# Rotary embedding by VectorE's lane shuffle in place of a rotation matrix on TensorE, in two of three chained transformer blocks

## The reference

```python
def apply_axial_rope(t, cos, sin):            # block 1: queries and keys
    tr = t.reshape(B, L, H, 2, 2, ROPE_PAIRS)  # ROPE_PAIRS = 16
    t1, t2 = tr[..., 0, :], tr[..., 1, :]
    out = jnp.stack([t1 * cs - t2 * sn, t2 * cs + t1 * sn], axis=-2)

def _rope(x, pos):                             # block 2: queries, compressed, selected and window keys
    x1, x2 = xf[..., :half], xf[..., half:]    # half = 32 of 64 channels
    return jnp.concatenate([x1 * cos - x2 * sin, x2 * cos + x1 * sin], axis=-1)
```

## Time and profile before

| | |
|---|---|
| times of three runs | 2611.19, 2609.15, 2611.22 us (median 2611.19) |
| profiled execution's own time | 2606.98 us |
| its span in the profile | 2605.2 us |
| busy PE, DVE, ACT, POOL | 2383.5 (91%), 1247.3 (48%), 976.5 (37%), 281.6 us (11%) |
| moved by the DMA queues | 884.58 MB, mean 340 GB/s |

### The profile page before, as it was taken

How to read it: one execution, slowest core, us unless ns; L and a number is a source line. 1 busy time by engine, 2 the same in 40 slices (tenths; PEclk the granted TensorE clock), 3 DMA queues, 4 the chain that set the end, 5 groups by cost and what they waited for, 6 DMA issues and landing times.

```text
span 2605.2 us, 43248 instructions
## 1 busy us (share of the span) xinstructions
PE 2383.5 (91%) x16141; PEld 1553.9 (60%) x16142; DVE 1247.3 (48%) x3094; ACT 976.5 (37%) x2122; POOL 281.6 (11%) x270
## 2 busy tenths in 40 slices
PE   7999989999999999999999998988778877799998
PEld 5679965555555545555568798443222322288997
DVE  2554542222222222222225757776666666557775
ACT  3343332112212121122124545554444444455774
POOL 0000000000000000000000001444434444200000
PEclk9999999999999999999999999999999999999999
DMA  6676699999999998999966655999999999833453
GB/s 271 263 262 252 228 358 417 422 422 422 421 422 422 422 422 355 422 422 422 422 236 266 258 226 218 422 421 421 421 422 421 421 421 422 361 133 138 162 185 139
DMA packets 121701, 884.58 MB, mean 340 GB/s; under 512 B 13536, under 2 KB 13536, under 8 KB 14304
## 3 DMA queue, kind: packets, MB, share of 16 engines
q1 hardware_dynamic: 83520, 607.16, 58.1%
q0 software_dynamic: 38048, 275.60, 25.5%
HBM read 881.66 MB, written 1.05 MB: 339 GB/s over the span
## 4 chain that ended last, share of the span: by engine, by line
PE 65%; DMA 22%; ACT 5%; DVE 3%; issue 2%; SPq 2%; POOL 0%; ACTq 0%; DVEq 0%; POOLq 0%
PE psum L840 15%; PE psum L1148 14%; DMA work<-in_uv,work 12%; PE psum L1526 8%; PE psum L1180 6%; DMA work<-in_stream 5%; DMA weight_ring<-in_stream 5%; PE psum L1619 2%; PE psum L1094 2%; PE psum L1115 2%; PE psum L693 2%; PE psum L863 2%; PE psum L913 2%; SPq L1689 2%; PE psum L753 1%
## 5 line engine op out<-in xcount | busy, mean ns | idle before, releaser
L1526 PE MATMUL psum<-work 128*128 128x512 f32 x1024 | 499.1, 620 | 116.9 <-ACT work L3302 116.0
L1526 PEld LDWEIGHTS psum<-work 128*128 128x128 f32 x1024 | 180.1, 192 | 426.8 <-ACT work L3302 273.0
L2503 DVE CUSTOM_DVE_ANT_0 work<-work 128x1024 f32<-128x1024 f32 x256 | 313.5, 1225 | 213.2 <-DMA work<-in_uv,work 211.9
L2144 DVE TENSOR_TENSOR work<-psum,work 128x256 f32<-128x256 f32 x132 | 56.0, 424 | 695.6 <-PE psum L1126 695.6
L1148 PE MATMUL psum<-work 128*64 128x256 f32 x3168 | 367.2, 383 | 17.3 <-DMA work<-in_stream 13.0
L1774 DVE TENSOR_TENSOR ring_parts<-weight_ring,peer_parts 128x1024 fp32r<-128x1024 f32 x218 | 261.4, 1221 | 200.6 <-ACT peer_parts L2935 155.3
L2935 ACT ACTIVATE peer_parts<-weight_ring 128x1024 fp32r<-128x1024 f32 x218 | 224.2, 1052 | 259.4 <-DMA weight_ring<-in_stream 157.2
L3492 POOL DMA_INDIRECT work<-in_uv,work x256 | 275.9, 1078 | 379.3 <-PE psum L1526 324.2
L1148 PEld LDWEIGHTS psum<-work 128*64 128x64 f32 x3168 | 220.6, 137 | 154.5 <-issue 29.3
L1180 PE MATMUL psum<-weight_ring,work 128*64 128x512 f32 x1056 | 244.2, 599 | 28.6 <-ACT work L3111 25.2
L3093 ACT ACTIVATE work<-psum 128x256 f32<-128x256 f32 x132 | 50.7, 384 | 366.9 <-PE psum L1148 366.9
(11 more groups left out here) (376 smaller groups left out, 3249.8 us busy)
## 6 DMA issues: line engine op xcount, KB each, us to landing
weight_ring<-in_stream SPq DMA_DIRECT2D x322, 1024.0 KB, 7.5
work<-in_stream SPq DMA_DIRECT2D x192, 1024.0 KB, 22.8
chunkbuf<-in_stream SPq DMA_DIRECT2D x64, 1024.0 KB, 22.7
work<-in_uv,work POOLq DMA_INDIRECT x256, 22.7
work<-in_rows POOLq DMA_DIRECT2D x1, 1312.0 KB, 15.0
xT<-in_x POOLq DMA_DIRECT2D x1, 1024.0 KB, 12.0
work<-in_ctx POOLq DMA_DIRECT2D x1, 1024.0 KB, 9.9
work<-in_keys POOLq DMA_DIRECT2D x1, 1024.0 KB, 7.5
```

Of the source, the lines that this page charges most:

```text
L1526: mm = pe.matmul(psum[:, 2 * t + h, :], m["diag"][:, g % DIAGS, :], m["rows_of_uv"][row_place[g]][:, D + h * 512:D + (h + 1) * 512], start ...
L2144: ve.tensor_tensor(tb, psum[:, 6, 0:256].rearrange("p (q k) -> p q k", q=4), m["b_gu"][:, slice(b0, b0 + 4) if q is None else bass.ds(b0, ...
L2503: ve.tensor_tensor_reduce(row, row, m["h_nat"][:, t, :], 1.0, 0.0, ALU.mult, ALU.add, m["score"][:, g:g + 1]).then_inc(pick_s, 1)
```

## The change

`rotate` and its matrix go. DVE's `rope` starts from `raw` directly: a stream shuffle writes `raw` into `t2` with lanes 0 to 15 and 16 to 31 of every 32 lanes swapped; `t1 = raw*cos` follows; then, after waits for DVE's own results, `t2 = t2*sin` and the sum. The minus sign is in the sine table. Since the shuffle stays within 32 lanes, block 2's head channels are put into another order (`paired`) on the host, in the weights that make the queries and keys and in the tables that go with them, so that partners there are 16 lanes apart too. Nine PE products of 128x512 or 128x256 go, and nine banks fewer are opened (five in block 1, four in block 2). The tables are 128 columns shorter in both blocks.

```diff
-    1: [("cos", T), ("sin", T), ("rot", P), ("mask", 2 * P), ...
+    1: [("cos", T), ("sin", T), ("mask", 2 * P), ...
+SWAPPED = [(lane + 16) % 32 for lane in range(32)]
...
-            def rotate(tag, E, m, raw, n0, n):
-                pe.wait_ge(*at(f"raw:{tag}"))
-                ps = bank(f"rot:{tag}")
-                pe.matmul(ps[:, 0:n * T], m["r"]["rot"], raw[:, n0:n0 + n, :], start=True, stop=True) \
-                  .then_inc(*E.up(f"rot:{tag}"))
...
                 for i in range(4):
                     columns_of_parts(1, "q1", i, m["h_high"], h_low)
-                    if i == 0:
-                        rotate("k1", E, m, m["kraw"], 0, 2)
-                    else:
-                        rotate(f"q1:{i - 1}", E, m, m["qraw"], 2 * (i - 1), 2)
-                rotate("q1:3", E, m, m["qraw"], 6, 2)
...
-                rotate("k2a", E, m, m["kraw"], 0, 2)
-                rotate("k2b", E, m, m["kraw"], 2, 1)
                 of_h = m["h_high"], h_low
                 pe.wait_ge(*at("high:h2"))
                 columns_of_parts(2, "hq", 0, *of_h, late="h2_parts")
-                for i in range(2):
-                    rotate(f"q2:{i}", E, m, m["qraw"], 2 * i, 2)
...
             def rope(tag, V, m, raw, dst, n0, n, *names):
-                ve.wait_ge(*at(f"rot:{tag}"))
+                ve.wait_ge(*at(f"raw:{tag}"))
                 wait_own(V)
-                ps = bank_of(f"rot:{tag}")[:, 0:n * T].rearrange("p (j t) -> p j t", j=n)
...
-                tt(V, m["t1"][:, 0:n, :], raw[:, n0:n0 + n, :], cos, ALU.mult)
-                tt(V, m["t2"][:, 0:n, :], ps, sin, ALU.mult, f"free:rot:{tag}")
+                t1, t2 = m["t1"][:, 0:n, :], m["t2"][:, 0:n, :]
+                ve.stream_shuffle(t2, raw[:, n0:n0 + n, :], SWAPPED).then_inc(*V.up())
+                tt(V, t1, raw[:, n0:n0 + n, :], cos, ALU.mult)
+                wait_own(V)
+                tt(V, t2, t2, sin, ALU.mult)
                 wait_own(V)
                 tt(V, dst[:, n0:n0 + n, :], m["t1"][:, 0:n, :], m["t2"][:, 0:n, :], ALU.add, *names)
...
-    return np.cos(angle).astype(np.float32), np.sin(angle).astype(np.float32), rot
+    sign = np.where(np.arange(P) % 32 < 16, -1.0, 1.0).astype(np.float32)
+    return np.cos(angle).astype(np.float32), np.sin(angle).astype(np.float32) * sign[:, None]
...
+    paired = n // 32 * 16 + n % 16 + n % 32 // 16 * 32
+    for k in ("kc", "ks", "kw"):
+        col[k] = col[k].reshape(D, NSA_G, HD)[:, :, paired].reshape(D, P)
```

More of the change, by code:

```diff
@@ L167 @@
 ROWS = {
-    1: [("cos", T), ("sin", T), ("rot", P), ("mask", 2 * P), ("b_v", 256), ("b_u", D), ("b_r", 32),
+    1: [("cos", T), ("sin", T), ("mask", 2 * P), ("b_v", 256), ("b_u", D), ("b_r", 32),
         ("iota", 32), ("seat", 2 * SEATS), ("w_r", DC * 32)],
-    2: [("cos", T), ("sin", T), ("rot", P), ("mask", P), ("cmp_mask", 2 * 16), ("reset", T),
+    2: [("cos", T), ("sin", T), ("mask", P), ("cmp_mask", 2 * 16), ("reset", T),
         ("hg_mask", 32), ("w_gl", DC * 24), ("w_ck2", HD), ("w_cv2", HD)],
@@ L3556, in everywhere, with rope_tables @@
     return np.broadcast_to(np.asarray(v).reshape(1, -1), (P, np.asarray(v).size))
[L3559 to L3566, removed]
-    return np.cos(angle).astype(np.float32), np.sin(angle).astype(np.float32), rot
+def rope_tables(angle):
+    sign = np.where(np.arange(P) % 32 < 16, -1.0, 1.0).astype(np.float32)
+    return np.cos(angle).astype(np.float32), np.sin(angle).astype(np.float32) * sign[:, None]
 def layout1(a):
@@ L3604, in layout1 @@
     pos = np.where((p[:, None] % 64) // 32 == 0, t[None, :] // 64, t[None, :] % 64).astype(np.float32)
-    cos, sin, rot = rope_tables(pos * inv[p % 16][:, None], 16)
+    cos, sin = rope_tables(pos * inv[p % 16][:, None])
     mask = np.concatenate([np.where(j <= i, 0, MASKED), np.where(j >= i, 0, MASKED)], 1).astype(np.float32)
-    W["rows"] = [cos, sin, rot, mask, everywhere(b_in[parts[2]]), everywhere(b_in[parts[3]]),
+    W["rows"] = [cos, sin, mask, everywhere(b_in[parts[2]]), everywhere(b_in[parts[3]]),
                  everywhere(a["b_router"][0]), everywhere(np.arange(32, dtype=np.float32)),
@@ L3627, in layout2, with compress @@
     perm = np.concatenate([np.arange(h * HD, (h + 1) * HD) for t in range(4) for h in (t, 4 + t)])
+    n = np.arange(HD)
+    paired = n // 32 * 16 + n % 16 + n % 32 // 16 * 32
+    for k in ("kc", "ks", "kw"):
+        col[k] = col[k].reshape(D, NSA_G, HD)[:, :, paired].reshape(D, P)
     def both(*n):
         return by_columns(np.concatenate([col[k] for k in n], 1))
-    def compress(w):
-        w = w.reshape(32, HD, P).transpose(1, 0, 2)
+    def compress(w, rows=slice(None)):
+        w = w.reshape(32, HD, P).transpose(1, 0, 2)[rows]
         w = np.concatenate([w, w], 0)
@@ L3644, in layout2 @@
     W["stream"] = [by_columns(a["w_ada_2"][0]), both("kc", "vc"), both("ks", "vs"), both("kw", "vw"),
-                   by_columns(col["q"][:, perm]), compress(a["w_ck1_2"][0]), compress(a["w_cv1_2"][0]),
+                   by_columns(col["q"][:, perm.reshape(8, HD)[:, paired].reshape(-1)]), compress(a["w_ck1_2"][0], paired), compress(a["w_cv1_2"][0]),
                    both("hq"), both("hf"), both("hi"), both("hg"), both("merge"),
@@ L3656, in layout2 @@
                 chan(a["g_final_2"]), np.full((P, 1), 1e-6, np.float32), chan(lb[0]), chan(lb[1]),
-                chan(a["hgrn_out_norm_2"][0]), pos(a["cmp_pos_k_2"][0]), pos(a["cmp_pos_v_2"][0]),
+                chan(a["hgrn_out_norm_2"][0]), pos(a["cmp_pos_k_2"][0][:, paired]), pos(a["cmp_pos_v_2"][0]),
                 everywhere(np.arange(PE_N, dtype=np.float32))]
@@ L3660, in layout2 @@
     inv = np.float32(10000.0) ** (-np.arange(32, dtype=np.float32) / np.float32(32))
-    cos, sin, rot = rope_tables(t.astype(np.float32)[None, :] * inv[p % 32][:, None], 32)
+    cos, sin = rope_tables(t.astype(np.float32)[None, :] * inv[p // 32 % 2 * 16 + p % 16][:, None])
     i, j = np.arange(P)[:, None], np.arange(P)[None, :]
@@ L3667, in layout2 @@
     w_gl = col["gl"].reshape(DC, P, 24).transpose(1, 0, 2).reshape(P, -1)
-    W["rows"] = [cos, sin, rot, np.where(j <= i, 0, MASKED).astype(np.float32),
+    W["rows"] = [cos, sin, np.where(j <= i, 0, MASKED).astype(np.float32),
                  cmp_mask.astype(np.float32).reshape(P, -1), reset, hg_mask.astype(np.float32), w_gl,
-                 a["w_ck2_2"][0], a["w_cv2_2"][0]]
+                 a["w_ck2_2"][0][:, paired], a["w_cv2_2"][0]]
     return W
```

## The result

The change is slower, by little: the median of 20 runs is 2615.82 us against 2611.82 us of 20 runs of the kernel before, ratio 1.0012 with a 95% interval of 1.0006 to 1.0017. The times of one kernel scatter by more than this difference (2610.32 to 2618.94 us with the change, 2608.98 to 2615.63 before); the interval is what tells the two apart. Forecast were 2606.9 us and a gain. Block 1 went as predicted; the loss lies at the entry of the expert loop, where PE stands still for a reason that the prediction did not have.

What follows compares the result with a forecast made beforehand. PE, 65% of the chain, was taken as the bound, VectorE's work costing only where PE waits. −4.3 + 1.4 − 0.9 − 0.5 = −4.3 us from the median 2611.19 gave 2606.9 us, range 2603.0 to 2611.0.

Steps and rivals of the forecast that it cites:

- Block 1: From the query products to values(0): values(0) starts at 105.9 us, a gain of 4.3 us.
- the hand-over: Block 1 to experts: gather(0) also waits for VectorE's reading of mod2, a loss of 1.4 us at most, at least 0.
- the half clock: Block 1, after PE's wait ahead of scores(2): the clock halves as after the old wait, costing 1.6 us.
- the rivals: Four: clock stays up or cheap shuffle 0.24; hand-over wait hidden 0.10; block 1's gain given back 0.14; slow shuffle 0.06.
- Other waits through banks I find none: Beyond gather(0), ks:0 and hg:0, no other wait through a bank's changed tenant was found; block 3 carries what is there.
- scores(0) without a wait: Block 1: PE's wait of 2.74 us for VectorE goes; scores(0) can start at 90.65 instead of 97.97 us.
- the new wait: Block 1, ahead of scores(2): PE waits 3.4 us, from 95.2 to 98.65 us, replacing the wait of 2.74.
- the ropes 2.90 apart for 2.84: VectorE in block 1: each rope takes 2.84 us instead of 2.12; four end at 95.5 us.
- rivals with a cheap or dear one: Shuffle at 0.44 us: −1.2, within the rival of chance 0.24; slow shuffle at 2.2 us: 2618.9 us, chance 0.06.
- Block 2's projections: Block 2 up to hf:0: a gain of 0.9 us, including ks:0's vanished bank wait of 0.66.
- the low halves of hf:0: Block 2: VectorE's longer ropes make PE wait here; they start at 1394.0 instead of 1392.06 us, PE goes on at 1395.2.
- −0.5: Block 2, hg:0: its bank wait of 0.53 us for VectorE goes, since the new tenant is read earlier.

Runs made afterwards that it cites:

- the first run: Changed kernel plus 25 never-executed instructions in PE's program, putting the expert loop's code where it was in the kernel before: 2610.61 us, ratio 0.9995.
- the second: Kernel before, rotations kept, plus 231 never-executed instructions, putting the loop's code where the change has it, by blocks of 256: 2616.79 us, ratio 1.0020.
- the fourth run: Changed kernel with loop code put back, second gather's bank opened behind the first gather, and block 3's mean of squares in bank 6: 2605.95 us, ratio 0.9983.
- the fifth: Changed kernel with code and two bank waits put right, plus block 2's k2a, k2b ropes and hq:0 low halves ahead of the gates' wait: 2601.69 us, ratio 0.9973.
- the twelfth: Changed kernel with 153 never-executed instructions in PE's program, so the loop's code begins in the middle of a block of 256: 2610.92 us, ratio 0.9997.
- The sixth: Changed kernel with code and two bank waits put right, plus ropes q1:2 and q1:3 moved behind the softmax of pairs 3 and 6: 2602.89 us, ratio 0.9970.
- the eleventh run: Changed kernel with loop code at its old place, plus the shuffle of block 1's four query tiles made twice: 2612.29 us, ratio 1.0004.
- the third run: Changed kernel with bank rotation moved on wherever a rotation's bank was opened, so later results keep their old banks; code not moved: 2611.92 us, ratio 1.0006.

## Why the prediction was wrong

**The step that failed is the hand-over**: "A loss of 1.4 us [...] At most it is that." The wait itself was 1.7 us; what it ended with, by the profile, is the amplitudes, made just behind `mod2`. But the jump into the loop lies behind it, and the change had shortened the code ahead of it; in the prediction's sum the jump has no term. I counted what PE executes and not where its code lies; the pause and the half clock cost 5.4 us in the profile. By the times, the first run puts it at 4.4 us (1.0012 less 0.9995) and the second at 5.2 (1.0020). None of the rivals had it.

**"Other waits through banks I find none"** was wrong by one: 0.97 us in block 3. With the one at gather(0) it is in the 3.1 us between the first and the fourth run.

**Block 1** held term by term: scores(0) without a wait, the new wait (3.67 us for 3.4), the ropes 2.90 apart for 2.84 (the shuffles of the last two query ropes start at 93.73 and 96.63), the half clock, 4.15 us for 4.3. The size of the half clock's term varies: from scores(2) to values(0) took 7.1 to 7.2 us in the change and four of the runs, but 8.35 and 8.14 in the fifth and the twelfth. The sixth and the eleventh run show that the ropes' end is what sets it: less in front gives the wait back, more makes it longer. The shuffle's spacing was 0.62 for 0.60, so that rivals with a cheap or dear one fall.

**Block 2's projections** gave 0.7 for 0.9, and PE waits at the low halves of hf:0, as forecast. The half clock behind the longer wait at `h_low`, 5.42 − 3.93 = 1.5 us, the prediction did not have; it cost nothing here, since VectorE's ropes set the start at hf:0 with it (57.67 us) and without it (57.65). In the eleventh run it lasted longer, and PE came to hf:0 0.8 us later (58.42).

**Gain and loss together**: −4.3 forecast and +1.0 for block 3's wait make −3.3 us for the change without the pause; with what the rows show for each term (−4.2 in block 1, +1.7, −0.7, −0.5, +1.0) it is −2.7. The first run measured −1.3 (interval −3.7 to +1.0), which holds both, and no gain at all too. By the ratios the change is 3.1 us slower than the kernel before and 4.4 slower than the first run; the 4.4 are the pause.

What stays open: in the profile of the change another 2.7 us went between 1500 and 1506 us, where PE had no wait and the clock was low (0.69 granted from 1500 to 1510, 1.00 in the same stretch before). The eleventh run has the like (0.70), and the shifted kernel before less of it (0.86); the first run has not (1.00). No run was made for it.

## What to carry to other kernels

Taking instructions out of one engine's program moves all its code behind; where a jump (a runtime branch, a loop's entry) follows, compare the idle time put down to "issue" behind it in both traces, and try a shift by instructions that are never executed before judging the change. A resource handed out in rotation does the same to waits: list each tenant and its last reader in both versions. And when work moves to an engine that had idle time, look for what can now start earlier: of the 9.9 us gained here in the end (0.9962), 5.5 came from a new order of VectorE's ropes. Whether the kernel before could have had part of that with its rotations on PE, no run shows.

## What the hardware showed unexpectedly

Where a loop's code lies can cost a second standstill of 2.9 to 3.1 us, 9 products behind the jump and its first standstill of 4.4 to 5.0: in three of three profiles with the loop's code at that place (the change, the second and the third run), and in none of the eleven with it elsewhere. The first 32 products take 10.0 to 10.5 us with it, and 4.9 to 6.5 without. The stream shuffle of 128x512 f32 took 0.72 to 0.77 us, little more than a product on that tile in the earlier trace rows, and its list of lanes 0.01 us.
